# Ten slots for expert weights in laps over eight experts, in a two-layer decoder trunk

## The reference

```python
def reference(x, ...):
    for layer in range(2):
        h = rms_norm(x, norm_mix_g[layer])
        mix = even_mixer(h, ...) if layer % 2 == 0 else odd_mixer(h, ...)   # proj = h @ w_in [1024, 3072]; ...; o @ w_out
        x = x + mix
        h = rms_norm(x, norm_ffn_g[layer])
        x = x + hier_moe(h, ...)
    return x

def hier_moe(h, ...):
    # top-1 group, top-2 experts in it, softmax weights; for each expert e, over its tokens xb:
    y = (jax.nn.silu(xb @ w_gate[e]) * (xb @ w_up[e])) @ w_down[e]          # each weight [1024, 1024]
    # y, weighted, is added to the tokens it came from
```

## Time and profile before

| | us |
|---|---|
| runs | 1234.75, 1227.23, 1238.0 |
| median | 1234.75 |
| profiled execution | 1236.96 |
| its span, first to last instruction | 1235.1 |

### The profile page before, as it was taken

How to read it: one execution, slowest core, us unless ns; L and a number is a source line. 1 busy time by engine, 2 the same in 40 slices (tenths; PEclk the granted TensorE clock), 3 DMA queues, 4 the chain that set the end, 5 groups by cost and what they waited for, 6 DMA issues and landing times.

```text
span 1235.1 us, 13944 instructions
## 1 busy us (share of the span) xinstructions
PE 1162.1 (94%) x5646; PEld 552.8 (45%) x5646; DVE 423.1 (34%) x748; ACT 189.9 (15%) x374; POOL 8.1 (1%) x36
## 2 busy tenths in 40 slices
PE   6997999999999999999989989899999999999988
PEld 5984453333333333333379855433333333333333
DVE  3746243322222232222266572532223223222223
ACT  3417210000000000000044161100001000000000
POOL 2000000000000000000000000000000000000000
PEclk9999999999999999999989999899999999999999
DMA  9665069999999999999984350799999999999996
GB/s 359 182 260 205 1 248 429 420 419 430 428 429 427 431 426 431 426 431 426 416 323 189 137 205 10 330 428 415 416 428 429 427 430 427 431 426 430 426 430 267
DMA packets 53904, 439.30 MB, mean 356 GB/s; under 512 B 14192, under 2 KB 14192, under 8 KB 29296
## 3 DMA queue, kind: packets, MB, share of 16 engines
q1 hardware_dynamic: 53872, 438.85, 85.8%
HBM read 437.79 MB, written 1.05 MB: 355 GB/s over the span
## 4 chain that ended last, share of the span: by engine, by line
PE 75%; DMA 18%; DVE 4%; ACT 2%; issue 1%; DVEq 0%; SPq 0%; ACTq 0%
PE bank L1493 42%; DMA ring<-in_moe_w_up 11%; PE bank L1382 8%; DMA ring<-in_moe_w_gate 6%; PE bank L1422 4%; PE bank L1471 4%; PE bank L1505 4%; PE bank L1377 3%; PE bank L1481 1%; PE bank L1536 1%; PE bank L1299 1%; PE bank L1210 1%; PE bank L1529 1%; PE bank L1392 1%; PE bank L1250 1%
## 5 line engine op out<-in xcount | busy, mean ns | idle before, releaser
L1493 PE MATMUL bank<-ring,qkT 128*64 128x512 f32 x2944 | 655.0, 597 | 27.9 <-DMA ring<-in_moe_w_gate 15.4
L1493 PEld LDWEIGHTS bank<-ring,qkT 128*64 128x64 f32 x2944 | 204.8, 137 | 453.8 <-issue 407.7
L1174 DVE TENSOR_SCALAR qkT<-qkT 128x512 f32<-128x512 f32 x32 | 13.7, 428 | 486.4 <-ACT qkT L748 486.4
L1176 DVE RECIPROCAL qkT<-qkT 128x512 f32<-128x512 f32 x32 | 107.3, 3353 | 1.1
L1505 PE MATMUL bank<-qkT 64*128 64x512 f32 x256 | 63.6, 615 | 5.6 <-ACT qkT L753 5.6
L1181 DVE TENSOR_TENSOR qkT<-bank,qkT 128x512 f32<-128x512 f32 x32 | 22.1, 692 | 131.7 <-PE bank L1493 131.7
L753 ACT ACTIVATE qkT<-bank 128x512 f32<-128x512 f32 x32 | 19.1, 597 | 304.3 <-PE bank L1493 304.3
L1422 PE MATMUL bank<-ring,hn 128*128 128x512 f32 x128 | 55.7, 593 | 1.2 <-ACT hn L663 0.7
L748 ACT ACTIVATE qkT<-bank 128x512 f32<-128x512 f32 x32 | 19.1, 598 | 243.2 <-PE bank L1493 243.2
L944 DVE TENSOR_TENSOR w_low<-ring,w_high 128x2048 fp32r<-128x2048 f32 x22 | 49.4, 2286 | 11.6 <-ACT w_high L596 11.6
L1471 PE MATMUL bank<-fn_high,take 128*128 128x512 f32 x136 | 47.8, 434 | 0.0
(11 more groups left out here) (214 smaller groups left out, 872.3 us busy)
## 6 DMA issues: line engine op xcount, KB each, us to landing
ring<-in_moe_w_gate SPq DMA_DIRECT2D x64, 2048.0 KB, 22.1
ring<-in_moe_w_down SPq DMA_DIRECT2D x64, 2048.0 KB, 24.9
ring<-in_moe_w_up SPq DMA_DIRECT2D x56, 2048.0 KB, 24.4
ring_spare<-in_moe_w_up SPq DMA_DIRECT2D x8, 2048.0 KB, 26.5
ring<-in_ab_w_in SPq DMA_DIRECT2D x12, 1024.0 KB, 14.1
ring<-in_c_w_in SPq DMA_DIRECT2D x12, 1024.0 KB, 14.7
ring<-in_ab_w_out SPq DMA_DIRECT2D x2, 2048.0 KB, 15.2
ring<-in_c_w_out SPq DMA_DIRECT2D x2, 2048.0 KB, 15.2
```

Source lines behind the costliest of these rows:

```text
L1176: nc.vector.reciprocal(sig, sig).then_inc(s.gate_step, 1)
L1493: last = mm(b[SLOTS * half:SLOTS * (half + 1), :], left(h, k), expert_rhs(slot, k, half), start=(h == 0 and k == 0), stop=(h == 1 and k == ...
```

## The change

The ring gets `RING = 9` slots, with the spare ten. The loop body covers eight experts (an "octet", 48 units), in laps of 10, 10, 10, 9 and 9 units, each lap from slot 0 upward; the spare is slot 9. A unit waits for the unit ten back in laps two to four, nine back in the fifth lap and in slots 0 to 8 of the next octet's first lap (slot 9 was free long before). TensorE, VectorE and ScalarE pass their loops twice in a layer, SyncE once, with the last octet's loads behind it. The new slot 8 is neither under `w_out` nor under `w_high`, and its first unit of each layer is loaded right behind `load_wout`, before the wait for `out_psum`.

The memory comes from two places: `dynamic_dma_scratch_size=1024`, and `cum` and `cum_neg` laid over `bias_a`. The matmuls, the order within an expert, and `giveT[k % 2]` are unchanged; the counters are renamed from quad to octet.

```diff
-RING = 8
+RING = 9
 SPARE = RING
-QUAD = 4
-QUAD_UNITS = QUAD * UNITS
-
-PLACES = [(SPARE, 0) if i == RING else ((i - (i > RING)) % RING, (i - (i > RING)) // RING)
-          for i in range(QUAD_UNITS)]
+OCTET = 8
+OCTET_UNITS = OCTET * UNITS
+
+LAPS = (10, 10, 10, 9, 9)
+SLOT_OF_UNIT = [slot for slots in LAPS for slot in range(slots)]
+PLACES = [(slot, SLOT_OF_UNIT[:i].count(slot)) for i, slot in enumerate(SLOT_OF_UNIT)]
+assert len(PLACES) == OCTET_UNITS and LAPS[0] == RING + 1
...
         w_high = [rounded(f"w_high{i}", [P, NC, COLS], ring_at[UNITS + i])
-                  for i in range(RING - UNITS)]
+                  for i in range(2)]
...
+        bias_at = nc.sbuf_base - 2 * A_HEADS * SW
+
+        def over_bias(name, n, at):
+
+            return nc.alloc_sbuf_tensor_at(name, [96, n], BF16, offset=bias_at + at)
...
-        cum = [sb(f"cum{i}", [96, T], BF16) for i in range(3)]
-        cum_neg = sb("cum_neg", [96, SW], BF16)
+        cum = [over_bias(f"cum{i}", T, 2 * T * i) for i in range(3)]
+        cum_neg = over_bias("cum_neg", SW, 6 * T)
...
                 load_wout(layer)
+                load_unit(layer, RING - 1, RING - 1 - UNITS, 1)
                 sp.wait_ge(s.out_psum, 4 * layer + 4)
-                for slot in range(UNITS, RING):
+                for slot in range(UNITS, RING - 1):
                     load_unit(layer, slot, slot - UNITS, 1)
...
-                with sp.Fori(0, last_quad) as quad:
-                    first = (quad & (N_EXPERTS // QUAD - 1)) * QUAD
-                    next_first = ((quad + 1) & (N_EXPERTS // QUAD - 1)) * QUAD
-                    for i in [*range(RING + 1, QUAD_UNITS), *range(RING + 1)]:
+                with sp.Fori(0, last_octet) as octet:
+                    first = (octet & (N_EXPERTS // OCTET - 1)) * OCTET
+                    next_first = ((octet + 1) & (N_EXPERTS // OCTET - 1)) * OCTET
+                    for i in [*range(RING + 1, OCTET_UNITS), *range(RING + 1)]:
...
-                with pe.Fori(0, last_quad + 1) as quad:
-                    for k in range(QUAD):
-                        now, after = turns(quad, k + 1), turns(quad, k + 2)
+                with pe.Fori(0, last_octet + 1) as octet:
+                    for k in range(OCTET):
+                        now, after = turns(octet, k + 1), turns(octet, k + 2)
...
-    nc = bacc.Bacc("TRN2", target_bir_lowering=False, num_devices=1)
+    nc = bacc.Bacc("TRN2", target_bir_lowering=False, num_devices=1, dynamic_dma_scratch_size=1024)
```

More of the change, by code:

```diff
@@ L364, in place, with turns, used @@
             return PLACES[UNITS * k + u]
-        def turns(quad, k):
-            return quad * QUAD + k
-        def used(s, quad, k, u):
+        def turns(octet, k):
+            return octet * OCTET + k
+        def used(s, octet, k, u):
             slot, lap = place(k, u)
-            return s.unit_used[slot], quad * USES[slot] + (lap + 1)
+            return s.unit_used[slot], octet * USES[slot] + (lap + 1)
         def spread_by(layer, j):
@@ L751, in _ @@
                         act.activation(giveT[k % 2], GATE[:, 0:T], ACT.Copy).then_inc(s.giveT_ready, 1)
-                        act.wait_ge(*used(s, quad, k, 5))
+                        act.wait_ge(*used(s, octet, k, 5))
                         act.activation(y_sb, Y[:, :], ACT.Copy).then_inc(s.y_ready, 1)
@@ L1165, in _ @@
                 dve.wait_ge(slots_ready, layer + 1)
[L1166 to L1173, removed]
+                last_octet = dve.value_load(last_octets[0:1, layer:layer + 1],
+                                          min_val=N_EXPERTS // OCTET - 1,
+                                          max_val=ROUNDS * N_EXPERTS // OCTET - 1)
@@ L1174, in _ @@
+                with dve.Fori(0, last_octet + 1) as octet:
+                    for k in range(OCTET):
+                        make_take(layer, turns(octet, k + 1))
+                        dve.wait_ge(s.gate_exp, turns(octet, k + 1))
                         ts(sig, sig, 1.0, None, ALU.add).then_inc(s.gate_step, 1)
-                        dve.wait_ge(s.gate_step, quad * (2 * QUAD) + (2 * k + 1))
+                        dve.wait_ge(s.gate_step, octet * (2 * OCTET) + (2 * k + 1))
                         nc.vector.reciprocal(sig, sig).then_inc(s.gate_step, 1)
-                        dve.wait_ge(s.gate_step, quad * (2 * QUAD) + (2 * k + 2))
+                        dve.wait_ge(s.gate_step, octet * (2 * OCTET) + (2 * k + 2))
@@ L1178, in _ @@
                         tt(sig, GATE[:, :], sig, ALU.mult).then_inc(s.gate_act, 1)
-                        dve.wait_ge(s.gate_act, turns(quad, k + 1))
-                        dve.wait_ge(*used(s, quad, k, 3))
+                        dve.wait_ge(s.gate_act, turns(octet, k + 1))
+                        dve.wait_ge(*used(s, octet, k, 3))
                         tt(hid, UP[:, :], sig, ALU.mult).then_inc(s.hid_ready, 1)
-                        leave_tokens(layer, turns(quad, k + 2))
-                        dve.wait_ge(s.hidT_psum, turns(quad, k + 1))
+                        leave_tokens(layer, turns(octet, k + 2))
@@ L1184, in _ @@
+                        dve.wait_ge(s.hidT_psum, turns(octet, k + 1))
                         nc.vector.tensor_copy(hidT, UP[:, :].rearrange("p (s t) -> p s t", s=SUB)
                                               ).then_inc(s.hidT_ready, 1)
-                        dve.wait_ge(s.giveT_psum, turns(quad, k + 1))
-                        make_give(layer, turns(quad, k + 1))
+                        dve.wait_ge(s.giveT_psum, turns(octet, k + 1))
+                        make_give(layer, turns(octet, k + 1))
@@ L1482, in tokens_out, with two_halves @@
                     last.then_inc(s.xt_psum, 1)
-                def two_halves(b, left, quad, turn, units):
+                def two_halves(b, left, octet, turn, units):
                     for h, u in enumerate(units):
                         slot, lap = place(turn, u)
-                        pe.wait_ge(s.unit_loaded[slot], quad * (USES[slot] * 16)
+                        pe.wait_ge(s.unit_loaded[slot], octet * (USES[slot] * 16)
                                    + ((WIN if slot < UNITS else 0) + 16 * (lap + 1)))
```

60 lines of the change are left out of this document (30 added, 30 removed).

## The result

| | us |
|---|---|
| before, median of 20 runs | 1234.33 (1227.23 to 1238.0) |
| changed, median of 20 runs | 1225.84 (1220.47 to 1230.77) |
| ratio | 0.9933, 95% interval 0.9921 to 0.9946 |
| profiled execution of the changed kernel, its span | 1228.05, 1226.3 |

The change brings 8.3 us by the ratio. It lies inside the range given, within 1% of the kernel before; the central value, 1222, took 12.8 us for the gain. So some two thirds of the forecast gain came, and the experiments look for the rest.

A forecast was written before the change was run, and what follows sets the result against it. The prediction took the DMA weight stream to bound the expert stages. One unit a layer (9.8 us) and closed gaps (3.0) took 12.8 us off 1236.96, so 1224.2, less 2.2 for the median: 1222 us, range 1214 to 1235.

The forecast's parts named there:

- What bounds the kernel: Expert stages: the end is the landing of a certain unit, set by the DMA stream at 4.9 us a unit.
- Part 1: Tenth slot's load falls into the idle attention stretch, so each layer's stage ends one unit earlier: 9.8 us.
- Part 2: Gaps in the early weight stream, at loads of units 18 and 24, close: 1.1 + 1.9 = 3.0 us.
- Part 3: Longer loop body: TensorE's own path 3.0 us shorter per layer, off the critical path; worth nothing; no jump stall.
- The rival on the stall: Jump back waits for a code fetch; costs time over 6.3 us, up to 1253.5 us; chance 0.07.
- The slack of Part 3: TensorE's waits for DMA left per layer after the change: 12.7 less 6.4, about 6.3 us.
- the rival's threshold of 6.3: A code-fetch stall at the jump costs nothing below 6.3 us, TensorE's slack per layer.
- Part 4: SyncE's single loop pass, `cum` over `bias_a` and the smaller scratch: priced at nothing.
- those named for a wrong forecast: Instruction transfers mid-stage with TensorE idle; a rate below 428; waits for DMA that vanish.
- one unit only: Stream dips are not the slots' doing, or the stream loses elsewhere: 9.8 us gain, 1225 us; chance 0.28.

The follow-up runs named there:

- Experiment 8: Changed kernel, but slot 8's first load stands behind the wait for the output projection, with slots 6 and 7; 1227.11 us, ratio 0.9955.
- experiment 7: Changed kernel, but units 10 to 47 of a layer wait for the unit the old ring made them wait for; 1235.65 us, ratio 1.0021.
- experiment 6: Kernel before, body of four experts, without the spare: eight slots in three full laps of eight; 1238.76 us, ratio 1.0044.
- experiments 2: Kernel before with most of TensorE's second column half of the expert matmuls left out, all weights still loaded; 1234.02 us, ratio 0.9999.
- experiment 3: Changed kernel with most of TensorE's second column half of the expert matmuls left out, about 1340 instructions in the body; 1222.18 us, ratio 0.9894.
- experiment 4: Changed kernel's ten slots with a body of sixteen experts, no jump back, SyncE's loop left out; 1221.45 us, ratio 0.9894; repeated 1222.26 us.
- experiment 9: Changed kernel with a hint ahead of the back jump on TensorE's loop; 1223.12 us, ratio 0.9925.
- experiment 1: Body of eight experts with the ring of the kernel before, eight slots and the spare; 1236.53 us, ratio 1.0022.

## Why the prediction was right or wrong

- **What bounds the kernel:** right for the kernel before. The end of a stage is the last landing plus fixed work. Nine slots against ten gave 10.0 us where the working had 9.8.
- **Part 1, the unit:** its size was right, its ground only in part. It was put down to the idle attention. Experiment 8 shows that the place of the load is a small matter, and experiment 7 that the distance at which a slot comes free is the large one.
- **Part 2, the gaps:** right. The dips went (429 GB/s), and experiment 6 found 1.0 and 1.9 us for them. Parts 1 and 2 together were given as 12.8 us, and experiments 2 and 3 measured 11.8 to 13.0.
- **Part 3, the longer body, priced at nothing:** this is the step that failed. The seam waits did halve. But the jump was argued from a body half as long; with the long one it cost TensorE 7.3 us in layer 0 and 12.6 in layer 1. The rival on the stall named this and held it for unlikely, because code read the first time stalls nothing. That was no evidence for a jump: in experiment 4, 45 transfers of code read in order stall no expert matmul either.
- **The slack of Part 3 was too small:** it took 6.3 us a layer from the waits that the view lists, 9.7. From the end of the first quad in layer 0 (281.38) to that of the last (616.87) are 335.5 us, where three quads at the free rate of 107.46 take 322.4: TensorE was held for 13.1 us. Layer 1 gives 13.3 (893.05 to 1228.72). So the slack after the change is 13.1 + 3.0 - 6.4 = 9.7 us, and the rival's threshold of 6.3 was too low. With 6.3 the stall of 7.3 us would have used up all waits for DMA in layer 0; 4.5 us of them stayed.
- **What no rival had:** code transfers and weights share the DMA engines, and a unit is as late as its slowest engine. From unit 30 to unit 93 the distance between first and last completion grew by at most 0.2 us in the four executions whose body stays resident (before, and experiments 2, 3 and 6) and by 0.7 to 2.7 us in the nine executions whose code is streamed. From the issue of the first load that waits for a use to the completions of unit 93 it takes, in us, layer 0 and layer 1, worked out from the semaphore updates:

```
kernel                        first            last
before                        419.1  419.8     421.7  422.4
changed                       413.3  413.6     417.9  418.4
body of 16 (experiment 4)     413.1  413.2     417.2  416.9
hint (experiment 9)           413.1  413.4     416.7  416.7
short code (experiment 3)     413.2  413.6     415.4  416.6
```

The first completion comes about 6 us earlier in every kernel of the table with ten slots, as Parts 1 and 2 have it (4.9 + 1.1 and 4.9 + 1.9). The last, which TensorE waits for, comes 3.8 and 4.0 us earlier in the changed kernel, 4.5 to 5.7 where code is streamed without a stall, and 6.3 and 5.8 where it stays resident. So both the jump and the streaming hold the last completion back, the streaming by 0.1 to 1.8 us a layer; these are single executions, and in the times only the jump's part is clear of noise. In layer 0 this was the loss: the stall fitted under the slack, and the last landing was 2.8 us earlier in place of some 6; 1.0 us of what is missing is a later start of the stage, 176.86 against 175.84, ahead of anything that the body of eight does.
- **In layer 1** both limits meet. The stall of 12.6 us is over the slack, no wait for DMA is left, and unit 93 lands at 1205.00, when TensorE comes to it: its row for u2 and u3 starts at 1201.31, and u3 is half of it:

```profile
1201.31 7.39 PE L1502 MATMUL bank<-ring,qkT 128*64 128x512 f32 x32
```

That stage went from 441.65 to 436.02 us (first to last start of the expert matmuls, L1493 before and L1502 after), but 1.7 of those 5.6 us are not the change's: its first GATE took 8.78 us before, where the granted clock was 0.66 from 785 to 790 us, and 7.09 after, at a granted clock of 1.00. Other executions with the change show either value.
- **Part 4:** nothing was seen of `cum` over `bias_a` or of the smaller scratch. None of them was tried alone, but experiment 3 has both and reaches the forecast.
- **The signs:** two of those named for a wrong forecast came, code transfers in the middle of a stage with TensorE idle, and in layer 1 waits for DMA that vanish.
- **The numbers:** the time, 1225.84 us, was in the range and lies beside "one unit only" (1225). That is chance: the gaps did close, and the body took back more than they were worth, some 4.5 us for 3.0.

What stays open is why a code transfer moves one completion for the rest of the stage, why the completions are 4.6 us apart at unit 30 in experiment 1's execution and 1.6 to 3.0 there in the others, and why the second octet's code was held in one pass with the hint and in no other.

## What to carry to other kernels

When a change unrolls a loop further, count the instructions of its body against the longest body that the trace shows to stay resident (no transfers of its code in the instruction queue after the first pass). Past that, expect a stall at the jump with a clock drop behind it; here a hint ahead of the jump, or a body without a jump, took both away. Each pass then also streams code through the engines that carry the data, which showed in the last completions. A ring is as deep as its shortest wait distance: look at the load that waits for the nearest use, not at the number of slots. When loads are split over many engines, look at the first and the last completion, for it is the last that wakes the consumer. When slack is counted, compare whole rounds with and without waits: here the listed waits were 9.7 us and the rounds lost 13.1.

## What the runs showed of the hardware

- A loop body of 1006 TensorE instructions was held over four passes; one of some 2000 was not held in the changed kernel, and was held in layer 1 with the hint. The stalls at the jump were 4.45, 4.51 and 4.63 us in the changed kernel.
- After a stall of that length the granted clock was at the 1.2 GHz level at once, and 32 matmuls took 9.9 us for 7.1.
- A 16 KB code transfer took about 1.0 to 1.2 us among the weights of the changed kernel's first expert stage, and could move the last of a unit's 16 completions by as much (3.5 to 4.5 us at unit 93 of layer 0).
- With a hint ahead of the jump the stall vanished altogether, and in one layer the second octet's code was not transferred at all.
